# Gate and up of a gated MLP in one sweep over k, with two of its eight block pairs by seven products instead of eight

## The reference, cut to what matters

```python
h = rms_norm(x, ffn_pre_g)
g = h @ w_gate                      # (256, 2048) @ (2048, 8192)
u = h @ w_up
g = conv_b + sum(shift(g, 2 - j) * conv_w[j] for j in range(3))   # causal, per column
y = (gelu(g) * u) @ w_down          # (256, 8192) @ (8192, 2048)
x = x + rms_norm(y, ffn_post_g)
```

## Time and profile before

| | |
|---|---|
| median of 3 runs | 1440.41 us (1440.12 to 1440.85) |
| profiled execution | 1440.96 us, span 1439.1 us |
| busy in the span | TensorE 1427.9, weight load 1191.1, VectorE 1055.1, ScalarE 741.6, GpSimd 361.1 us |
| DMA | 293.28 MB, mean 204 GB/s |

### The profile page before, as it was taken

One profiled execution on the slowest core, in us unless ns is written; L12 is line 12 of the kernel. 1 busy time (PEld: TensorE's weight loads), 2 busy tenths in 40 slices (PEclk: granted clock), 3 DMA queues, 4 the chain that ended last, 5 costly groups with the idle time before them and its releaser, 6 DMA issues.

```text
span 1439.1 us, 20247 instructions
## 1 busy us (share of the span) xinstructions
PE 1427.9 (99%) x6598; PEld 1191.1 (83%) x6598; DVE 1055.1 (73%) x1629; ACT 741.6 (52%) x935; POOL 361.1 (25%) x609
## 2 busy tenths in 40 slices
PE   9999999999999999999999999999999999999997
PEld 9888888888878888888888888888888888888886
DVE  6867678966576656666656666656767999989897
ACT  7455544554565444444444444444445666656663
POOL 0701010720013433434424424424424000000000
PEclk9999999999999999999999999999999999999999
DMA  7655656555568777777777777777777666656553
GB/s 263 220 187 150 195 184 190 163 168 178 179 191 235 220 211 222 217 213 219 217 217 219 217 210 221 221 211 221 214 220 234 205 206 211 217 185 202 194 193 113
DMA packets 149670, 293.28 MB, mean 204 GB/s; under 512 B 17232, under 2 KB 30832, under 8 KB 149360
## 3 DMA queue, kind: packets, MB, share of 16 engines
q1 hardware_dynamic: 132416, 274.71, 62.7%
q0 software_dynamic: 16384, 16.81, 3.8%
q10 hardware_dynamic: 816, 1.09, 0.2%
HBM read 273.67 MB, written 2.10 MB: 192 GB/s over the span
## 4 chain that ended last, share of the span: by engine, by line
PE 92%; issue 4%; DVE 1%; DMA 1%; POOL 1%; ACT 0%; SPq 0%; DVEq 0%; POOLq 0%; ACTq 0%
PE psum L1730 21%; PE psum L1734 21%; PE psum L1732 21%; PE psum L1958 17%; PE psum L1697 3%; PE psum L1941 2%; PE psum L1939 2%; PE psum L1940 2%; PE psum L1701 1%; DMA stage<-in_w_qkv 1%; PE psum L1778 0%; PE psum L1784 0%; PE psum L1715 0%; POOL sq_sum L943 0%; PE psum L1621 0%
## 5 line engine op out<-in xcount | busy, mean ns | idle before, releaser
L1031 DVE TENSOR_TENSOR w_lo<-stage,w_hi 128x1024 fp32r<-128x1024 f32 x381 | 469.0, 1233 | 320.3 <-ACT w_hi L591 319.4
L591 ACT CAST w_hi<-stage 128x1024 fp32r<-128x1024 f32 x381 | 400.7, 1053 | 532.6 <-PE psum L1734 496.0
L1730 PE MATMUL psum<-w_hi,hT 128*128 128x512 f32 x1272 | 498.3, 392 | 0.0
L1734 PE MATMUL psum<-w_hi,hT 128*128 128x512 f32 x1272 | 495.2, 389 | 0.0
L1732 PE MATMUL psum<-w_lo,hT 128*128 128x512 f32 x1272 | 495.1, 389 | 0.0
L1734 PEld LDWEIGHTS psum<-w_hi,hT 128*128 128x128 f32 x1272 | 238.7, 188 | 49.9
L1730 PEld LDWEIGHTS psum<-w_hi,hT 128*128 128x128 f32 x1272 | 238.8, 188 | 49.5 <-DVE hT L1060 0.3
L1732 PEld LDWEIGHTS psum<-w_lo,hT 128*128 128x128 f32 x1272 | 238.8, 188 | 49.1
L1958 PE MATMUL psum<-w_hi,hT 128*128 128x512 f32 x704 | 191.2, 389 | 0.0
L1003 POOL DMA_DIRECT2D up_rows_f<-up_T x256 | 137.1, 545 | 213.4 <-DVE up_T L1378 181.2
L1003 POOL DMA_DIRECT2D gate_rows_f<-gate_T x256 | 134.9, 536 | 209.2 <-DVE gate_T L1378 177.4
(11 more groups left out here) (201 smaller groups left out, 1451.8 us busy)
## 6 DMA issues: line engine op xcount, KB each, us to landing
stage<-in_w_gate SPq DMA_DIRECT2D x128, 512.0 KB, 3.7
stage<-in_w_up SPq DMA_DIRECT2D x128, 512.0 KB, 3.8
stage<-in_w_qkv SPq DMA_DIRECT2D x93, 512.0 KB, 3.7
stage<-in_w_down SPq DMA_DIRECT2D x86, 512.0 KB, 4.6
stage_wide<-in_w_down SPq DMA_DIRECT2D x42, 512.0 KB, 4.1
stage<-in_w_o SPq DMA_DIRECT2D x32, 512.0 KB, 3.9
gate_rows_f<-gate_T POOLq DMA_DIRECT2D x256, 32.0 KB, 3.3
up_rows_f<-up_T POOLq DMA_DIRECT2D x256, 32.0 KB, 3.2
```

The lines of the kernel that those rows point to most:

```text
L591: nc.scalar.copy(w_hi[s][:, :], stage[s][:, :]).then_inc(s_hi, 1)
L1031: nc.vector.tensor_tensor(w_lo[s][:, :], stage[s][:, :], w_hi[s][:, :].bitcast(F32), ALU.subtract).then_inc(s_lo, 1)
L1730: nc.tensor.matmul(o, lo[:, k, ts], w_hi[s][:, w], start=(k == 0), stop=False, skip_group_check=True)
L1734: ins = nc.tensor.matmul(o, hi[:, k, ts], w_hi[s][:, w], start=False, stop=last and kk == 1, skip_group_check=True)
```

## The change

Iteration 0 stays as it was. For iterations 1 to 15 gate and up are one sweep over k: block q of group G (iteration G + 1) is k tiles 2q and 2q+1 against 512 columns of gate beside 512 columns of up. That has the form of a block of down, and the same code serves both: `blocks` lists 15 groups of 8 blocks and then down's 2 passes of 32. Blocks 2 and 4 of each group are summed. The loop over iterations is gone, everything is written out.

- Loads: for a block of these groups SP waits for both of its stages, then loads gate's half (columns 0 to 511 of both stages) and up's half; ScalarE's cast of either stage waits for both loads.
- Rows: the sums of the normed rows for k pairs 2 and 4 are made once, in iteration 0 (`normed_sums`, `normed_sum_low` on VectorE, `normed_sum_high` on ScalarE), into `h_sums`, in the memory of `post_g`.
- Weights: three sums per summed block on VectorE (`sums_of_weights`), into `scratch` and `factors`.
- Banks: direct and p banks change places with each group. TensorE waits for the joint products of the group before at each group's block 0, and for its adds at the first summed block.
- Results: ScalarE takes one p bank out (`take_first_product`), VectorE does four joint products at the end of the group, from PSUM to `gate_rows_f` and `up_rows_f`, and four adds after blocks 0 and 1 of the next; ScalarE scales by the RMS factor in place (`scale_rows`).
- Gating steps stand at other units: with n = 2q + j, VectorE adds gate after n = 1 and up after 2, turns gate after 3, turns up after 7, taps after 10, 11, 13, product with up after 15; ScalarE scales after 3 and does the GELU after 14. They are done in place for the last iteration in pass 0 of down as well.
- Down: summed k pairs 8, 10, 13, 15, 17, 20, 22, 25, 27, 29 in pass 0 and 4, 6, 9, 11, 14, 16, 19, 21, 24, 27 in pass 1: ten each.

The core of the diff:

```diff
-SUMMED = ((7, 9, 12, 14, 17, 20, 23, 26, 29), (4, 7, 10, 13, 16, 19, 22, 25, 27))
+F_GROUPS = F_ITERS - 1
+D0 = F_GROUPS * CHUNK_UNITS
+F_SUMMED = (2, 4)
+SUMMED = ((8, 10, 13, 15, 17, 20, 22, 25, 27, 29), (4, 6, 9, 11, 14, 16, 19, 21, 24, 27))
...
+        GATE_ADD_AT, UP_ADD_AT, ACT_SCALE_AT, GATE_TURN_AT, UP_TURN_AT = 1, 2, 3, 3, 7
+        CONV_AT, GATED_AT, ACT_GELU_AT = (10, 11, 13), 15, 14
...
-        blocks = [(p, q) for p in range(PASSES) for q in range(PAIRS)]
+        blocks = ([(G, q) for G in range(F_GROUPS) for q in range(CHUNK_UNITS)]
+                  + [(F_GROUPS + p, q) for p in range(PASSES) for q in range(PAIRS)])
...
-            with sp.Fori(1, F_ITERS) as i:
-                load_ffn(i)
...
+            for g, (G, q) in enumerate(blocks):
+                if g < D0:
+                    wait_for_unit(2 * g)
+                    wait_for_unit(2 * g + 1)
+                    dst = pair_stage(g).rearrange("p (a n) -> p a n", a=2)
+                    for c, rows in enumerate((gate_rows, up_rows)):
+                        sp.dma_start(dst[:, :, c * CHUNK:(c + 1) * CHUNK],
+                                     rows[:, 2 * q:2 * q + 2, (G + 1) * CHUNK:(G + 2) * CHUNK]
+                                     ).then_inc(s_stage[stage_of[2 * g + c]], 16)
...
+            def scale_rows(i, c):
+
+                rows, signal = ((gate_rows_f, s_gate_row), (up_rows_f, s_up_row))[c]
+                for t in range(TT):
+                    act.wait_ge(s_y_sum, (i - 1) * (2 * TT) + c * TT + t + 1)
+                    nc.scalar.activation(rows[:, t, :], rows[:, t, :], ACT.Copy,
+                                         scale=rms_row[:, t:t + 1]).then_inc(signal, 1)
...
-                act.wait_ge(s_stage[stage_of[u]], 16 * loads_of[u])
+                for load in (2 * g, 2 * g + 1) if g < D0 else (u,):
+                    act.wait_ge(s_stage[stage_of[load]], 16 * loads_of[load])
...
+            def take_first_product(G):
+
+                act.wait_ge(s_used, block_used(ENDS[G]))
+                if G < F_GROUPS:
+                    act.wait_ge(s_conv, (G + 1) * (2 * CT))
+                nc.scalar.copy(y_of(G, 0, 0), p_bank(G, 0)[:, :]).then_inc(s_p1, 1)
...
+            def sums_of_weights(g):
+
+                before = [h for h in range(g) if is_summed(h)]
+                if before:
+                    dve.wait_ge(s_lo, block_used(before[-1]))
+                else:
+                    dve.wait_ge(s_h_sum, 4 * len(F_SUMMED))
+                    dve.wait_ge(s_h_sum_lo, len(F_SUMMED))
+                weight_sum_13(g)
+                weight_sum_2(g)
+                weight_sum_4(g)
...
+            def gating_steps(i, n):
+
+                if n == GATE_ADD_AT and i > 0:
+                    add_rows(i, 0)
+                if n == UP_ADD_AT and i > 0:
+                    add_rows(i, 1)
+                if n == GATE_TURN_AT and i > 0:
+                    turn_gate(i)
+                if n == UP_TURN_AT:
+                    turn_up(i)
...
+                if n == GATED_AT:
+                    gated_rows(i)
...
-            with pe.Fori(1, F_ITERS) as i:
-                ffn(i)
...
-            for g, (p, q) in enumerate(blocks[:FINAL]):
+            for g, (G, q) in enumerate(blocks[:FINAL]):
+                if q == 0 and G > 0:
+                    pe.wait_ge(s_joint, 4 * G)
+                if q == SUMS[G][0]:
+                    if G > 0:
+                        pe.wait_ge(s_y_sum, 4 * G)
...
+                if is_summed(g):
                     summed_block(g)
                 else:
                     plain_block(g)
```

More of the change, by code:

```diff
@@ L242, in layer_kernel @@
         Q_BANK, V_BANK, WARM_BANK, S_BANK, O_BANK = 0, 2, 5, 6, 7
+        SUMS_AT = tuple(10 + 2 * x for x in range(len(F_SUMMED)))
+        GATE_ADD_AT, UP_ADD_AT, ACT_SCALE_AT, GATE_TURN_AT, UP_TURN_AT = 1, 2, 3, 3, 7
+        CONV_AT, GATED_AT, ACT_GELU_AT = (10, 11, 13), 15, 14
         PAIR = 2 * P
@@ L413, in layer_kernel @@
             first_slot.append(len(slot_of))
-            for v in range(first_slot[g], first_slot[g] + (4 if summed else 2)):
+            for v in range(first_slot[g], first_slot[g] + (4 if is_summed(g) else 2)):
                 s, free = in_turn.pop(0)
@@ L452, in unit_stage, with pair_stage, w_sum_of, a_sums_before @@
             return stage[stage_of[u]]
+        def pair_stage(g):
+            s = stage_of[2 * g]
+            return (stage_all[:, s * UNIT:(s + 2) * UNIT] if s < RING
+                    else stage_wide[:, (s - RING) * UNIT:(s - RING + 2) * UNIT])
         def quarters(g):
[L456 to L459, removed]
+            return pair_stage(g).rearrange("p (b n) -> p b n", b=4)
+        def w_sum_of(g):
+            return w_sum_ffn if g < D0 else w_sum_down
         def sums_before(g):
[L463 to L471, removed]
+            return sum(is_summed(h) for h in range(g))
+        def a_sums_before(g):
+            return sum(is_summed(h) for h in range(D0, g))
+        def c_bank(G, t, c):
+            return bank[4 * ((G + 1) % 2) + 2 * t + c]
+        def p_bank(G, n):
+            return bank[4 * (G % 2) + n]
         x_rows = x.rearrange("(t p) d -> p t d", p=P)
@@ L1455, in _ @@
                     low_part((F_START + n) // RING, n % RING)
+                if n in SUMS_AT:
+                    normed_sum_low(SUMS_AT.index(n))
                 if n == 12:
                     turn_gate(0)
[L1459 to L1472, removed]
+                if n + 1 in SUMS_AT:
+                    normed_sums(SUMS_AT.index(n + 1))
             def gated_low(g):
@@ new lines, in scale_by_gain @@
+                nc.vector.tensor_tensor(y_of(F_GROUPS + p, t, c), src, ffn_g[:, cs], ALU.mult).then_inc(s_d_out, 1)
+            for g, (G, q) in enumerate(blocks):
+                if is_summed(g):
+                    if g >= D0:
+                        sums(g)
+                        gated_low(g)
+                        unit_low(g, 0, CHUNK)
+                        gated_sum_low(g)
+                    else:
+                        sums_of_weights(g)
+                        unit_low(g, 0, CHUNK)
@@ new lines, in rows_of, with summed_rows_of, rows_product @@
+            def rows_of(g, part):
+                q = blocks[g][1]
+                return hT[:, 2 * q:2 * q + 2, part, :] if g < D0 else (a_hi, a_lo)[part](entry[g])
+            def summed_rows_of(g, part):
+                q = blocks[g][1]
+                return h_sums[:, F_SUMMED.index(q), part, :, :] if g < D0 else (a_hi, a_lo)[part](entry[g] + 1)
+            def rows_product(o, rows, g, w, cs, j, ts, start):
+                hi, lo = rows(g, 0)[:, j, ts], rows(g, 1)[:, j, ts]
+                nc.tensor.matmul(o, lo, w_hi[w][:, cs], start=start, stop=False, skip_group_check=True)
+                nc.tensor.matmul(o, hi, w_lo[w][:, cs], start=False, stop=False, skip_group_check=True)
+                return nc.tensor.matmul(o, hi, w_hi[w][:, cs], start=False, stop=False, skip_group_check=True)
@@ L1963, in summed_block @@
             def summed_block(g):
-                p, q = blocks[g]
-                e, v = entry[g], first_slot[g]
-                start = q == SUMMED[p][0]
+                G, q = blocks[g]
+                v = first_slot[g]
+                start = q == SUMS[G][0]
                 t0, t1 = ROWS
```

387 lines of the change are left out of this document (212 added, 175 removed).

## The result

The changed kernel takes 1433.23 us (median of 5 runs, 1432.08 to 1435.55), the kernel before 1440.74 in the same series: a ratio of 0.9949, 95% interval 0.9938 to 0.9960. It is 7.5 us faster, where 18.1 were forecast, and above the range of 1418.6 to 1426. The direction was right.

The account below looks back on a forecast made before the run. The number of matmuls on TensorE was taken to set the time: 21.8 us saved less stalls of 3.0, 0.5 and 0.2 gave 18.1, so 1422.3 us on the median. Its own range was 1418.6 to 1426; 8 in 10, 1418.5 to 1431.

Parts of the forecast that it names:

- Matmuls removed, and their price: Iterations 1 to 15 lose 90 matmuls and down 6, at 0.2267 us each: 21.8 us saved.
- VectorE's sum: VectorE's work per iteration after the change: 40.9 us of the 42.16 that TensorE needs, 97%.
- The chain to the next group's slot 0: From block 4 through tap 0, GELU and slot 19 to the next group: ready at 42.1, due 42.16, slack 0.0 to 0.1.
- Loads: A pair's two 512 KB loads land in 5.5 us, within 5.2 to 5.8 available; no stall at the mean.
- second estimate: Pair landing by the Trainium skill's figure: 6.2 us, 0.2 beyond block 4's slack, kernel near 1427.
- the wait at 21.08: Block 4's last two slots wait for TensorE to end block 3, 21.08 us into the iteration; said to catch each delay.
- Block 4: Second summed block of each group: its second slot ready at 21.45, due 21.76, least slack 0.3 us.
- Hand-over to a waiting TensorE: TensorE can start some 1.27 us after VectorE began the low part, range 1.25 to 1.40.
- Down: Down projection: 0.5 us of stall once at its first block, 0.2 in pass 0, none in pass 1.
- Loads late: Rival: late pair loads stall block 4 each iteration; 1434 at 7.0 us landing, 1427 at 6.3; chance 0.17.
- The slower side: Rival: even blocks' stage hand-around loop exceeds the iteration; at 8.0 us landing about 1510 us; chance 0.04.
- The signs: Wrong if TensorE's named waits sum to over 8 us, loads land beyond 6.3, or pass 0 waits exceed 2 us.

Follow-up runs that it names:

- the best version: Changed kernel with four 256 KB loads per pair, each stage for itself, and the GELU after slot 19's cast: 1418.59 us, 0.9846 of the kernel before.
- half loads: Changed kernel with each load in iterations 1 to 15 bringing only its pair's first k tile, 256 KB instead of 512 KB: 1422.51 us.
- four loads: Changed kernel with four 256 KB loads per pair, each stage loaded when it alone is free, each cast waiting for its own stage: 1423.60 us.

## Why the prediction was wrong, by its steps

- **Matmuls removed, and their price: right.** 96 less; with the waits gone the kernel is 22.0 us faster, 21.8 were counted.
- **VectorE's sum: right.** 40.9 us of 42.16 per iteration forecast, 611.9 / 15 = 40.8 of busy time measured (95% of the longer stretch; 97% in the best version).
- **The chain to the next group's slot 0: the place right, the size wrong.** This is the step that failed, as the term "0.2 us of stall per iteration (between 0 and 0.5), 3.0 in all". It was 14.9 / 15 = 1.0. The prediction had tap 0 end 33.7 us into the group and the GELU follow at once, with block 7's load 0.3 of spare time beside it. Measured on average: tap 0 ends at 34.44 and the GELU starts at 34.54. The larger part of this comes from block 4's loads, by way of VectorE, the smaller from slot 18's (0.9 us in all). The chain as walked, without the loads' part, is what half loads and four loads show, with 0.2 us at the end: had the loads been on time, the forecast of 1422.3 would have stood (1422.5 and 1423.6).
- **Loads: the landing right on average, wrong for block 4, and its use wrong.** 5.5 us for a pair was the estimate; the second load's median 5.1 plus 0.41 for its later issue is 5.5. But block 4's pair took longer: its second load landed 5.2 to 7.1 us after its issue, median 5.7, so 6.1 for the pair. The 5.7 us up to its first use and the spare 0.3 behind them were used up, with SP's wake-up (0.08) and the hand-over (0.07 for a cast) on top. The prediction's second estimate, 6.2, was the nearer one. Why this pair is slower, no run shows. I wrote that the delays "don't add up with the others, since each is caught by the wait at 21.08". The runs show the opposite. VectorE comes to slot 13, where that wait stands, 0.5 us later on average than with half the load, so the wait catches little; the delay is still there at tap 0, a place whose slack I had put at 0.0 to 0.1. And low 15, late by about as much, frees slot 18's stage late, so the same delay also goes round VectorE over the stage, the load and ScalarE's order, as the run without tap 1 shows.
- **Block 4: slack 0.3 and "no stall at the mean": wrong by 5.0 us**; 2.1 are left when only the GELU is moved, none with half the load.
- **Hand-over to a waiting TensorE:** 1.27 taken, 1.37 measured (784.49 to 785.86).
- **Down: 0.5 and 0.2 of stall.** The entry lost 1.0, pass 0 0.4. By itself down loses nothing that its profile shows.
- **The rivals.** None of them as it was put is what happened. "Loads late" came nearest: it had the place (block 4) and, at 6.3 us of landing, 1427, but it counted only block 4's own stall (5.0 measured) and not what the same loads do to the first slots: 9.1, of which 3.5 are left with half the load. Its prices also don't follow one rule: by the sum that gives 1434 at 7.0, a landing of 6.3 gives 1424, and without the deduction of 0.2 a landing of 6.2 gives 1425, not 1427. The slower side was within reach by another mechanism than the one named: the GELU one cast earlier costs 17 us.
- **The signs.** The first sign of being wrong came: waits of 14.9 us, where 8 was the limit. The second came in part: three of the 14 block-4 pairs landed beyond 6.3 us, at most after 7.5. Pass 0 of down stayed under its 2 us.

A remainder is small: counted savings less the measured waits (14.9 in the groups, 0.4 in down) are 6.5 us, the kernel gained 7.5. In the profiles the first group starts at 441.47, where iteration 1 of the kernel before started at 442.39 (counted back from down), 0.9 us later; no experiment looked for the reason.

## What to carry to other kernels

An instruction with a late operand holds all that stands behind it in its engine's queue: put it behind the last instruction that feeds a tighter consumer, even if its own result then comes later. Two places with 0.3 us of spare time each are no margin when one feeds the other; walk the loop of buffer, load, cast and queue order as one chain. An engine without pauses carries a delay on until something gives it time back. Two loads that share a joint wait cost the earlier half its head start; four loads, each stage for itself, gave 10 us back for the same bytes. And look at every group before you name the wait that counts: slot 18's load, which ended last in the group shown, did so in only four of 14.

## What the runs showed of the hardware

- Two 512 KB loads issued 0.41 us apart: the second lands after 5.1 us (median of 128), where single ones took 3.8 before; in four parts of 256 KB the medians are 3.1 and 3.9. For the same pair of each group the second took 5.2 to 7.1 us.
- A low part of 1024 columns starts 1.37 us before the first matmul that waits for it (duration 1.22). The matmul behind the released one starts another 0.08 us late (0.11 at block 4), so a wait costs TensorE about 0.1 us beyond its own length.
- TensorE's page share says little here: 98.8% busy in the changed kernel's iterations (636.97 of 644.50) went with 2.3% of lost time (14.9 of 647.3).
